# A hybrid attention trunk: mixer B's tiles and steps in another order with the gates last, and all low parts of y made by VectorE

## What is computed

```
h = rmsnorm(x);  aq, ak, av, ag, bq, bk, bv, bg = split(h @ w_in)     # 2048 -> 6400 columns
ya = chunked attention of 16 heads with a relative bias(aq, ak, av) * silu(ag)      # mixer A
qb, kb = rope(bq), rope(bk)
yb = sliding-window attention of 16 heads, 2 key-value heads, with sinks(qb, kb, bv) * silu(bg)   # mixer B
x = x + concat(ya, yb) @ w_out                                       # 2048 -> 2048
```

## Time and profile before

| | |
|---|---|
| median of 3 runs | 1680.85 us (1680.38 to 1681.51) |
| the profiled execution | 1679.48 us, span 1677.7 us, mean granted clock 0.993 |
| TensorE matmul busy | 1634.7 us, 97% |
| VectorE busy | 956.4 us, 57% |
| ScalarE busy | 840.9 us, 50% |
| GpSimd busy | 128.8 us, 8% |

### The profile page before, as it was taken

The page is one execution under the profiler, slowest core; times in us unless marked ns, Lnnn a source line. Parts: engine busy times, 40 slices in busy tenths (PEclk is TensorE's granted clock), DMA queues, the critical chain, the costliest instruction groups (busy, mean ns, idle before and its releaser), DMA issues.

```text
span 1677.7 us, 24250 instructions
## 1 busy us (share of the span) xinstructions
PE 1634.7 (97%) x7688; PEld 1355.8 (81%) x7688; DVE 956.4 (57%) x2009; ACT 840.9 (50%) x1867; POOL 128.8 (8%) x99
## 2 busy tenths in 40 slices
PE   7999999999999998999999999999999999989996
PEld 6888888888888786888888888888888888768885
DVE  6555555555567777433455555555556676773334
ACT  7555555555545556322345555556555655552221
POOL 2000000000211112100000000000002111120000
PEclk9999999999999999999999999999999999999998
DMA  6323222222223222444332232213223222223333
GB/s 230 103 87 112 77 85 87 99 99 87 88 88 114 82 89 88 151 149 139 120 119 76 89 110 87 94 71 109 87 87 120 88 88 82 84 106 137 125 117 139
DMA packets 41026, 175.69 MB, mean 105 GB/s; under 512 B 5456, under 2 KB 7792, under 8 KB 24192
## 3 DMA queue, kind: packets, MB, share of 16 engines
q1 hardware_dynamic: 40928, 174.81, 30.5%
q0 software_dynamic: 32, 0.08, 0.0%
HBM read 161.68 MB, written 8.47 MB: 101 GB/s over the span
## 4 chain that ended last, share of the span: by engine, by line
PE 80%; DVE 8%; issue 6%; ACT 4%; POOL 1%; DVEq 0%; ACTq 0%; POOLq 0%
PE ps_proj L453 23%; PE ps_proj L455 23%; PE ps_proj L454 23%; PE ps_o L515 2%; PE ps_t L505 2%; DVE w_lo L977 2%; ACT probs L758 1%; PE ps_s L497 1%; PE ps_s L496 1%; DVE probs L1054 1%; ACT w_hi L676 1%; DVE temp L989 1%; DVE xy L1097 1%; PE ps_s L530 1%; DVE xy L1398 1%
## 5 line engine op out<-in xcount | busy, mean ns | idle before, releaser
L453 PE MATMUL ps_proj<-act_hi,w_hi 128*128 128x512 f32 x2048 | 810.8, 396 | 18.2 <-DVE act_lo L978 8.7
L455 PE MATMUL ps_proj<-act_hi,w_lo 128*128 128x512 f32 x2048 | 801.2, 391 | 0.0
L454 PE MATMUL ps_proj<-act_lo,w_hi 128*128 128x512 f32 x2048 | 799.7, 390 | 0.0
L977 DVE TENSOR_TENSOR w_lo<-w_raw,w_hi 128x512 fp32r<-128x512 f32 x532 | 384.4, 737 | 247.1 <-ACT w_hi L676 238.4
L453 PEld LDWEIGHTS ps_proj<-act_hi,w_hi 128*128 128x128 f32 x2048 | 386.0, 188 | 94.2 <-DVE act_lo L978 8.7
L455 PEld LDWEIGHTS ps_proj<-act_hi,w_lo 128*128 128x128 f32 x2048 | 385.6, 188 | 83.6
L454 PEld LDWEIGHTS ps_proj<-act_lo,w_hi 128*128 128x128 f32 x2048 | 386.4, 189 | 73.5
L676 ACT ACTIVATE w_hi<-w_raw 128x512 fp32r<-128x512 f32 x532 | 315.7, 620 | 258.5 <-PE ps_proj L455 250.6
L742 ACT ACTIVATE probs<-probs,nmax 128x128 f32<-128x128 f32 (+3 forms) x128 | 71.9, 562 | 111.5 <-DVE nmax L1040 109.1
L676 ACT ACTIVATE probs<-probs,rden 128x128 f32<-128x128 f32 (+3 forms) x128 | 72.1, 563 | 106.5 <-DVE rden L1061 106.5
L1249 DVE TENSOR_TENSOR xy<-ps_proj,temp 128x512 f32 (+1 forms) x30 | 20.8, 692 | 171.8 <-PE ps_proj L455 171.8
(11 more groups left out here) (89 smaller groups left out, 1197.8 us busy)
## 6 DMA issues: line engine op xcount, KB each, us to landing
w_raw<-w SPq DMA_DIRECT2D x131, 1024.0 KB, 4.8
temp<-temp SPq DMA_DIRECT2D x72, 64.0 KB, 3.9
strips<-ext SPq DMA_DIRECT2D x16, 256.0 KB, 5.8
temp<-xT SPq DMA_DIRECT2D x16, 256.0 KB, 2.6
xs<-xy SPq DMA_DIRECT2D x16, 256.0 KB, 2.4
temp<-xs SPq DMA_DIRECT2D x16, 256.0 KB, 2.6
out<-xy SPq DMA_DIRECT2D x16, 256.0 KB, 2.3
strips<-ext SPq DMA_DIRECT2D x16, 224.0 KB, 5.8
```

The lines of the kernel that those rows point to most:

```text
L453: pe.matmul(dst, wh, act_hi[:, k, :], start=start, stop=False)
L454: pe.matmul(dst, wh, act_lo[:, k, :], start=False, stop=False)
L455: return pe.matmul(dst, wl, act_hi[:, k, :], start=False, stop=stop)
L977: return nc.vector.tensor_tensor(dst, src, hi, ALU.subtract)
```

## The change

1. The 14 tiles behind mixer B's first four come in the order `TILES_B`: q2 q3 g0 q4 q5 g1 q6 q7 g2 g3 g4 g5 g6 g7.
2. Steps are scored at P2, 5, 8, 11, 15, 18, 21, 24, 28, 31, 34, 37, 41, 44, 47, 50 instead of 1, 4, 7, 10, 15, 18, 21, 24, 29, 32, 35, 39, 45, 47, 50, 53.
3. ScalarE splits both query pairs of a group in one point (12, 25, 38), VectorE in that point and the next. Before it was 11 and 12, 27 and 28, 43 and 44.
4. ScalarE splits the point's weights behind the copy of the low scores and ahead of the exponentials, where it did so behind them.
5. Gates use t_gate alone, and y is gated at the points `GATED_AT`.
6. All low parts of y are made by VectorE; GpSimd makes none. High and low parts are made at P53 (k 0, 1), P54 (2, 3), P56 (4 to 7), P57 (8, 9), P58 (10, 11), P59 (12, 13), P60 (14, 15), where they were made at P54 (0 to 3), P55 (4 to 7), P57 (8 to 11), P58 (12, 13), P59 (14, 15).
7. The second output tile's weights are split chunk by chunk as the last input tile's quarters are projected: P55, 57, 58, 59 instead of P56, 57, 58, 59.

```diff
-SCORES_B = (1, 4, 7, 10, 15, 18, 21, 24, 29, 32, 35, 39, 45, 47, 50, 53)
+SCORES_B = (2, 5, 8, 11, 15, 18, 21, 24, 28, 31, 34, 37, 41, 44, 47, 50)
+TILES_B = (("q", 2), ("q", 3), ("g", 0), ("q", 4), ("q", 5), ("g", 1), ("q", 6), ("q", 7),
+           ("g", 2), ("g", 3), ("g", 4), ("g", 5), ("g", 6), ("g", 7))
+Q_AT = (12, 25, 38)
+GATED_AT = (16, 25, 37, 41, 45, 49, 55, 57)
...
 # ScalarE
-            def softmax_b(L, n):
+            def softmax_b(L, n, other):
                 act.wait_ge(s_done, step_b(L, n) + 1)
                 for dst, src in low_scores(n):
                     last = copy(dst, src)
                 last.then_inc(s_low, 1)
+                other()
                 act.wait_ge(biased, step_b(L, n) + 1)
...
+            def phase_b(L, T, points, split):
+                for point in points:
+                    if point == 0:
+                        hi_q_b(L, 1, t_k)
+                    attend_b(L, point, lambda: split(point))
+                    if point == 1:
+                        hi_v_b(L * V_LAYER + PAIRS)
+                    if point in Q_AT:
+                        for i in range(2):
+                            hi_q_b(L, Q_AT.index(point) * 2 + 2 + i, t_queries(i))
+                    if point and point % PTS == 0:
+                        kind, b = TILES_B[point // PTS - 1]
+                        if kind == "g":
+                            gate(tile_b(T, "g", b), t_gate)
...
+                def weights(point):
+                    split_w(T + (A_SLOTS + 4), point // PTS + 1, point % PTS)
+                    if point == 53:
+                        hi_ys(0, 2)
+                    if point == 54:
+                        hi_ys(2, 4)
+                    if point == 55:
+                        split_w(O, 1, 0, rows)
+
+                def last_weights(point):
+                    if point == 56:
+                        hi_ys(4, 8)
+                    if 57 <= point < 60:
+                        split_w(O, 1, point - 56, rows)
+                        hi_ys(8 + (point - 57) * 2, 10 + (point - 57) * 2)
+                    if point == 60:
+                        hi_ys(14, 16)
+                    if 60 <= point < 63:
+                        split_w(O, 2, point - 60, parts)
...
 # VectorE
+            def phase_b(L, T, points, split):
+                B = T + (A_SLOTS + 4)
+                for point in points:
+                    if point == 0:
+                        dve.wait_ge(q_done, pair_b(L, 1))
+                        take(B, -1, t_v)
+                        lo_q_b(L, 1, t_k)
+                    elif point % PTS == 0 and point <= POINTS_B:
+                        s = point // PTS - 1
+                        kind, b = TILES_B[s]
+                        if kind == "g":
+                            take(B, s, t_graw, 0.5)
+                        else:
+                            take(B, s, t_queries(b))
+                    attend_b(L, point)
+                    split(point)
+                    if point == 1:
+                        lo_v_b(L * V_LAYER + PAIRS)
+                    for i in range(2):
+                        if point - i in Q_AT:
+                            lo_q_b(L, Q_AT.index(point - i) * 2 + 2 + i, t_queries(i))
+                    if point % PTS == 1 and 1 < point <= POINTS_B + 1:
+                        kind, b = TILES_B[point // PTS - 1]
+                        if kind == "g":
+                            gate(pair_b(L, b))
+                    if point in GATED_AT:
+                        gated_b(L, GATED_AT.index(point))
...
 # GpSimd
-                for k in range(0, KT, 2):
-                    pool.wait_ge(y_hi_done, L * KT + (k + 1))
-                    nc.gpsimd.tensor_tensor(act_lo[:, k, :], xy[:, k, :], act_hi[:, k, :].bitcast(F32),
-                                            ALU.subtract).then_inc(y_lo_done[0], 1)
```

More of the change, by code:

```diff
@@ L412, in _ @@
                         swap(L, s - 1, T + (A_SLOTS + s - 1), t_q if s == 2 else t_k)
[L413 to L419, removed]
+                for s in range(len(TILES_B)):
+                    prefetch(T + (A_SLOTS + 4), s)
+                    if s > 0 and TILES_B[s - 1][0] == "q":
+                        b = TILES_B[s - 1][1]
+                        swap(L, b + 1, queries_tile(T, b), t_queries(b))
                 sp.wait_ge(q_done, pair_b(L, PAIRS))
@@ L790, in attend, with attend_b @@
                     other()
-            def attend_b(L, point):
+            def attend_b(L, point, other=lambda: None):
                 for n in at_point(point, VALUES_AT):
@@ L796, in attend_b @@
                     hi_p_b(L, n)
-                for n in at_point(point, 0):
-                    softmax_b(L, n)
+                scores = at_point(point, 0)
+                for n in scores:
+                    softmax_b(L, n, other)
+                if not scores:
+                    other()
             def square(L, j, half, par):
@@ L939, in hi_y, with hi_ys @@
                     copy(act_hi[:, k, :], xy[:, k, :]).then_inc(y_hi_done, 1)
-                def hi_ys(p):
-                    for k in {6: range(0, 4), 7: range(4, 8), 9: range(8, 12), 10: (12, 13), 11: (14, 15)}.get(p, ()):
+                def hi_ys(first, last):
+                    for k in range(first, last):
                         hi_y(k)
[L945 to L958, removed]
+                def weights(point):
[6 more added lines that the diff above has]
+                        split_w(O, 1, 0, rows)
+                phase_b(L, T, range(POINTS_B), weights)
+                def last_weights(point):
[8 more added lines that the diff above has]
+                        split_w(O, 2, point - 60, parts)
+                phase_b(L, T, [POINTS_B], lambda point: None)
+                for point in range(POINTS_B, POINTS_B + 7):
+                    last_weights(point)
+                split_w(O, 2, PTS - 1, parts)
                 square(L + 1, 0, 0, 0)
@@ L1348, in _, with lo_ys @@
                 unit(T + A_SLOTS, L, att_a(L, PAIRS - 1), PAIRS - 1, ("b", None, None))
-                for D in range(UNITS_B - 1):
-                    unit_b(L, T, D, 4, lambda p: None)
                 O = T + IN_TILES
-                def lo_ys(p):
-                    for k in {6: (1, 3), 7: (5, 7), 9: (9, 11), 10: (13,), 11: (15,)}.get(p, ()):
+                def lo_ys(first, last):
+                    for k in range(first, last):
                         dve.wait_ge(y_hi_done, L * KT + (k + 1))
-                        low(act_lo[:, k, :], xy[:, k, :], act_hi[:, k, :].bitcast(F32)).then_inc(y_lo_done[1], 1)
@@ L1358, in _ @@
[L1358 to L1375 removed]
+                        low(act_lo[:, k, :], xy[:, k, :], act_hi[:, k, :].bitcast(F32)).then_inc(y_lo_done, 1)
@@ L1376, in _ @@
+                phase_b(L, T, range(POINTS_B), weights)
+                phase_b(L, T, range(POINTS_B, POINTS_B + 7), last_weights)
                 residual(L, 0, 0, 0, O)
@@ L1467, in tile_columns @@
     cols += [bk, bq, bq + P, bv]
[L1468 to L1470 removed]
+    cols += [(bq if kind == "q" else bg) + b * P for kind, b in TILES_B]
     return cols
```

163 lines of the change are left out of this document (51 added, 112 removed).

## The result

The changed kernel takes 1654.64 us (median of 4 runs, 1654.31 to 1654.99) where the kernel before took 1681.18 beside it (1680.38 to 1682.57): ratio 0.9841, 95% interval 0.9824 to 0.9858. A second measurement gave 1655.90 against 1680.14, ratio 0.9860 (0.9842 to 0.9877). Over all executions of this study the medians are 1680.1 (43 executions, 1676.6 to 1683.8) and 1655.2 (8, 1654.3 to 1656.8): 24.9 us, 1.5%. The forecast was 1660.0, with a range of 1655 to 1670. It was right about where the time goes, and the gain is larger than it said.

What follows compares the result with a forecast made beforehand. TensorE, busy 97% of the span, bounds the kernel, so only its stops and half-clock time can be won: 21.3 us gone, 1.2 new, half of 1.6 in short pauses gone, 20.9 off 1680.85 gives 1660.0 us; range 1655 to 1670.

Steps and rivals of the forecast that it cites:

- the new stop: P28, third group's first score: low query 0.6 us late; 1.2 us of new cost over both layers.
- A: Queries still late at P15, P28 and P41: 9.9 us stand instead of 1.2, total 1668.7; chance 0.13.
- C: Mixer B's step chain outlasts its 3 points and stops TensorE each step: 35 us cost, total 1695; chance 0.05.
- B: Handover stop only changes its name, y 4 onwards late: 11 us come back, total 1671.0; chance 0.12.
- The warning about the rope: GpSimd's rope operations beside mixer B's steps may each hold VectorE for 1.3 us, twice a step; nothing added.
- The bracketed stops: TensorE's named waits in mixer B and handover, 8.3 us in layer 0, 0.7 less in layer 1; all counted as gone.
- The short pauses: Unbracketed TensorE pauses at a turn, values and a product: up to 0.8 us a layer, half of 1.6 gone.
- The clock: Behind the handover's weight wait, half of a 3.3 us stretch at 1.2 GHz is lost: 1.7 us a layer, gone.
- The query waits: TensorE's mixer B waits for low parts of rotated queries: 3.2 us in layer 0, 2.5 in layer 1.
- The steps themselves: Mixer B's sixteen steps a layer: new spacing and weight split ahead of exponentials gain nothing on TensorE, taken as 0.
- the account of P24 to P28: Engine times through mixer B's densest place, P24 as zero: low query done at 13.3, P28 at 12.7, 0.6 late.
- Slack 2.4 us: Handover: second output tile's first low chunk ready at 3.5 after P55 starts, P57 needs it at 5.9; wait goes.

## Why the prediction was right about the place and short in size

**The stops and what removes them.** Right, each one: no wait for w_lo, act_lo or the multiply, no half clock between the layers' mixer B and the output tiles, and the new stop in the place it was given, with 0.64 and 0.65 us lost for the 0.6 worked out. The low query ends 13.3 us after P24 begins, as worked out. Rivals A and C did not come about; B neither: y 4 to 7 hang on take and tanh, and their first low part is ready 1.8 us ahead of P58.

The warning about the rope came true on VectorE and cost nothing. In the second profile of the changed kernel beside GpSimd's rope operations at 543.42 and 544.80 (1.29 and 1.28 us), the add at 543.57 takes 1.17 us instead of 0.16 and the multiply at 544.98 takes 1.65 instead of 0.69; the multiply still ends at 546.6, and its turn starts at 547.97 without a wait. The chain had the cover.

**The sum is 4.1 us short.** The step that failed is the sizing of its terms; the path was right. The four profiles of before lose 26.2 us a piece in the two mixer stretches (24.9 more than the changed kernel, and its own 1.3); I credited 22.1. The bracketed stops of the profile that I read were right: 17.9 credited, 17.9 lost between starts. Four other sizes were too small:

- The short pauses. The term is "half of the unbracketed 1.6", 0.8; they were 1.9 and all went: 1.1 short.
- The restart, for which the sum has no term. Behind a stop the second matmul starts 0.34 us after the first, not 0.23, and scores at a stop spread out by 0.1; over the stops of two layers that is 1.1.
- The clock, "half of that stretch's work is lost, 1.7 us", taken as a fixed price from one profile. Over the four profiles five handovers cost 1.6 or 1.7, three 2.4 to 2.6, and one query stop 1.7: 4.3 us an execution where 3.4 stood, 0.9 short.
- The query waits, 5.7 us in the one profile, 6.4 on average over four: 0.7 short.

That is 3.8 of 4.1; the rest is spread too thin to place. The forecast of 1660.0 is a further 0.7 high because it starts from 1680.85, the median of three runs, where 43 executions have 1680.1. The first measurement's difference of 26.5 us has its part of chance as well: the kernel before ran at 1681.18 there, 1 us above that median.

**The steps themselves.** Here the prediction was wrong in its reasoning, though not in its sum. "Spare time there buys nothing" put the split ahead of the exponentials at 0. It is worth 8.1 us alone and 9.6 when taken back. That the total came out near is in part luck: the sum counted stops by place, and the account of P24 to P28 already had the split in its new place, so the size was inside the 21.3 us. A reader of that paragraph would have left the edit out and lost a third of the gain or more.

**The chunk at the handover.** "Slack 2.4 us" was right for the chunk and wrong for P57, which also needs the take. The cover is 0.9 us (take done at 5.0, P57 at 5.9), and the text had both numbers without putting them together. The early chunk alone, worth 8 us by that reasoning, gave 2.2.

**Attribution.** Alone, the parts gave 4.0, 2.2 and 8.1, sum 14.3; together 15.9; with y 4 to 7 behind the take 20.0; with the new order of tiles and steps 24 to 25. Of that last part, the order of tiles, the points of the scores, the two queries in one point and the points of the gating were only tested together.

## What to carry to other kernels

A wait names what came last, not what else was late: list everything that the waiting point needs, and find each in its engine's queue. An engine that waits a little in every step is late everywhere; look at how far behind its partner it enters the dense places. Price the clock behind a stop, and every stop that varies, from several profiles, and take from a stretch at half clock what lies in the stop itself. Count short pauses and slow restarts too: here they were 3 us of 26.

## What the runs showed of the hardware that I had not expected

- An idle time of 3.6 or 3.7 us of TensorE at the handover came with 3.4 us at 1.2 GHz in five cases and with 6.8 us in three, in the same kernel with the same stop. In the three, the clock had fallen 1.4 to 2.0 us before TensorE went on.
- The length of an idle time alone doesn't decide whether the clock falls. Behind 1.83 us at 1388.2 in one profile of before, and behind 2.90 us at 1378.1 in the kernel with the split behind, there were 3.4 us at 1.2 GHz; behind 2.23 us in layer 0 of the latter (at 563.4), 1.49 us at 567.94 and the 1.7 us waits for the take it stayed up.
- With its operations between GpSimd's, a 4-element add of VectorE took 1.27 us instead of 0.16, and a 128x512 operation 1.59 to 1.78 instead of 0.69. The delay is about as long for the small one as for the large.
